# Weight loads one unit later in the order of the DMA queue, and FoX stack pieces at one per step of a product

## What is computed

```python
def first_block(x, ...):
    h = rmsnorm(x, ln1)
    u_pool, gq, gk, gv, gg, ga, fq, fk, fv, ff = split(h @ w_in)
    y_pool = pool_mixer(u_pool, w_pool, pool_scale)            # trailing means
    y_gla = gla_mixer(gq, gk, gv, gg, ga, w_a_up, b_a, gla_gn) # chunked gated linear attention
    y_fox = fox_mixer(fq, fk, fv, ff, b_f)                     # softmax(qk + F_t - F_s), causal, 8 heads of 64
    x = x + concat(y_pool, y_gla, y_fox) @ w_o
    gate, up = split(rmsnorm(x, ln2) @ w_gu)                   # 2 x 2816
    x = x + (silu(gate) * up) @ w_down
    return rmsnorm(x, ln_f)

def second_block(x, ...):
    (q_lat, c_kv, k_rope, z_a, q_b, k_b, v_b, z_b,
     q_idx, k_idx, w_idx, gate_a, gate_b) = split(rmsnorm_2(x, norm_g) @ w_in_2)
    y_a = mla_attention(...) * silu(z_a)   # from the normed latents q_lat and c_kv
    score = sum over heads of w_idx * relu(q_idx . k_idx)   # top 128 keys of each query
    y_b = dsa_attention(...) * silu(z_b)   # attention over those keys, with a T5 bias
    merged = sigmoid(gate_a) * (y_a @ w_o_a) + sigmoid(gate_b) * (y_b @ w_o_b)
    return rmsnorm_2(x + merged @ w_out, final_g)
```

## Time and profile before

| | |
|---|---|
| runs | 1107.45, 1107.36, 1106.17 us; median 1107.36 |
| the profiled execution | 1106.37 us, of which the span of the trace is 1104.6 |
| granted TensorE clock over the span | 0.988 of full speed |
| PE busy | 1050.1 us (95% of the span), 5160 matmuls |
| DVE, ACT, POOL busy | 623.3, 469.3, 256.6 us |
| chain of work that ended last | PE 73%, DVE 14%, ACT 6%, issue 4% |
| loads of weights | 162 of 512 KB, 3.4 us median from issue to landing |

### The profile page before, as it was taken

How to read it: one execution, slowest core, us unless ns; L and a number is a source line. 1 busy time by engine, 2 the same in 40 slices (tenths; PEclk the granted TensorE clock), 3 DMA queues, 4 the chain that set the end, 5 groups by cost and what they waited for, 6 DMA issues and landing times.

```text
span 1104.6 us, 13494 instructions
## 1 busy us (share of the span) xinstructions
PE 1050.1 (95%) x5160; PEld 843.1 (76%) x5160; DVE 623.3 (56%) x1048; ACT 469.3 (42%) x815; POOL 256.6 (23%) x155
## 2 busy tenths in 40 slices
PE   7799889899999999999999998799999999999996
PEld 5597677667888888888888776577787766788885
DVE  6755577747454433344444556898756665425544
ACT  6634346546322222132334465545764554423322
POOL 0581332222101000011113323422323223321100
PEclk9999899999999999999999999999999999999998
DMA  8031132212223232223233326212222423122222
GB/s 293 4 122 50 39 117 78 78 58 77 96 96 96 98 131 77 94 83 109 93 100 94 110 70 209 85 39 74 60 88 78 118 91 104 59 96 96 99 73 77
DMA packets 34655, 102.32 MB, mean 93 GB/s; under 512 B 4544, under 2 KB 8016, under 8 KB 34592
## 3 DMA queue, kind: packets, MB, share of 16 engines
q1 hardware_dynamic: 34592, 101.47, 28.3%
HBM read 93.35 MB, written 4.74 MB: 89 GB/s over the span
## 4 chain that ended last, share of the span: by engine, by line
PE 73%; DVE 14%; ACT 6%; issue 4%; SPq 2%; DMA 1%; DVEq 0%; POOL 0%; ACTq 0%; POOLq 0%
PE bank L1352 20%; PE bank L1354 20%; PE bank L1353 20%; PE bank L1484 2%; PE bank L1475 2%; PE bank L1364 1%; DVE m L2038 1%; DVE score L2029 1%; PE bank L1366 1%; PE bank L1365 1%; DVE score L2040 1%; ACT WH L1537 1%; DVE f_s L1828 1%; DVE small L1922 1%; PE bank L1456 1%
## 5 line engine op out<-in xcount | busy, mean ns | idle before, releaser
L1352 PE MATMUL bank<-HH,WH 128*128 128x512 f32 x808 | 330.1, 409 | 16.9 <-DVE WL L1784 8.3
L1354 PE MATMUL bank<-HH,WL 128*128 128x512 f32 x808 | 317.8, 393 | 0.0
L1353 PE MATMUL bank<-HL,WH 128*128 128x512 f32 x808 | 317.4, 393 | 0.0
L2115 POOL TENSOR_TENSOR WL<-WS,WH 128x1024 fp32r<-128x1024 f32 x64 | 154.8, 2419 | 358.1 <-ACT WH L1537 357.7
L1352 PEld LDWEIGHTS bank<-HH,WH 128*128 128x128 f32 x808 | 154.2, 191 | 54.4 <-DVE WL L1784 8.3
L1537 ACT ACTIVATE WH<-WS 128x1024 fp32r<-128x1024 f32 x162 | 168.6, 1047 | 56.5 <-PE bank L1354 41.5
L1354 PEld LDWEIGHTS bank<-HH,WL 128*128 128x128 f32 x808 | 153.1, 189 | 33.4
L1353 PEld LDWEIGHTS bank<-HL,WH 128*128 128x128 f32 x808 | 153.8, 190 | 29.5 <-issue 1.0
L1784 DVE TENSOR_TENSOR WL<-WS,WH 128x1024 fp32r<-128x1024 f32 x98 | 130.3, 1335 | 25.9 <-ACT WH L1537 25.9
L2168 POOL TENSOR_TENSOR fa<-fa,fg 128x512 f32<-128x512 f32 x22 | 28.3, 1285 | 273.4 <-DVE fa L1975 273.4
L1352 PE MATMUL bank<-GH,WH 128*128 128x512 f32 x176 | 68.5, 389 | 0.0
(11 more groups left out here) (339 smaller groups left out, 1749.7 us busy)
## 6 DMA issues: line engine op xcount, KB each, us to landing
WS<-wall SPq DMA_DIRECT2D x162, 512.0 KB, 3.4
scratch<-rows SPq DMA_DIRECT2D x8, 320.0 KB, 5.6
X<-xT SPq DMA_DIRECT2D x8, 256.0 KB, 6.2
b_t<-scratch SPq DMA_DIRECT2D x8, 256.0 KB, 3.8
outT<-X SPq DMA_DIRECT2D x8, 256.0 KB, 2.1
b_m<-b_m SPq DMA_DIRECT2D x11, 128.0 KB, 4.1
f_s<-f_s SPq DMA_DIRECT2D x8, 128.0 KB
f_m<-f_m SPq DMA_DIRECT2D x8, 128.0 KB
```

The lines of the kernel that those rows point to most:

```text
L1352: e.matmul(b[:, :], wh, xh[:, at_k, :], start=k == 0, stop=False)
L1353: e.matmul(b[:, :], wh, xl[:, at_k, :], start=False, stop=False)
L1354: m = e.matmul(b[:, :], wl, xh[:, at_k, :], start=False, stop=k == n - 1)
L2115: e.tensor_tensor(WL[:, u % NW, :], WS[:, u % NST, :], f32(WH[:, u % NW, :]), ALU.subtract).then_inc(*tick(w_low_g, u))
```

## The change

Two edits. The load of unit u+3 no longer stands at step "split u" in SP's order, but at step "split u+1". Its own wait, for `split_low(u)`, and its buffer stay as they are. And `now["per"]` is not raised to 2.0 behind the gate products: it stays at 1.0 until it is set to 0.0 at the end of FoX.

```diff
@@ build, FoX @@
         run(gate_products())
-        now["per"] = 2.0
         behind.append(fox_stack(1))
         behind.append(gla_out())
@@ sync_program @@
                 elif kind == "split":
-                    load(s["u"] + NST)
+                    if s["u"]:
+                        load(s["u"] - 1 + NST)
                 elif kind == "forget":
```

## The result

The changed kernel takes 1113.91 us (median of 6 runs, 1112.80 to 1116.18); the kernel before, run beside it, 1107.49 us (6 runs, 1106.17 to 1110.57). The ratio is 1.0057, 95% interval 1.0041 to 1.0072: 6.3 us slower, between 4.5 and 8.0. The forecast was 1114.2 us, 1108 to 1120, and slower with 0.79.

A forecast was written before the change was run, and what follows sets the result against it. TensorE, busy 1050.1 of 1104.6 us, was taken as the bound, so only its waits count. 1106.4 + 12.5 (load 104) - 3.4 (DSA copies) - 0.3 (FoX wait) - 1.0 (pieces) = 1114.2 us, range 1108 to 1120.

The forecast's parts named there:

- The block of 31 issues: Between splits 101 and 102 on SP: load 104 goes out behind 24 index and 7 key copies, everything behind 12.5 us later.
- The direct stall of PE: PE waits before the token sums for the copy of the index weights queued behind split 104 on ACT: 7.4 us.
- the bounds: For load 104's delay: 7.4 us if only the direct stall counts, 13.7 if ACT makes nothing good.
- The small copies of DSA: PE's waits at 891.39 and 924.44 go, as copies no longer queue behind loads: 3.4 us gained (0 to 3.95).
- FoX's wait of 0.28 us: PE's wait at 145.05 goes: 0.3 us gained.
- The pieces: FoX, stack pieces at 1.0: 4.0 us gained at f_v, Pb and PT, 3.0 lost; together -1.0 us.
- the new waits: PE waits for stacks 2 and 3 at logits (4,0) and (6,0) in FoX: 1.5 us each, 3.0 in sum.
- The range of -6.5 to +4: Range in us given for the pieces' -1.0, from a gain of 0 to 6.5 and a loss of 0 to 7.
- Load 8: Waits for three copies of the forget rows, lands near 51: costs nothing, or some 4 us without cover.
- the cover: ACT's next split waits 7.83 us for load 9, until 57.31, anyway, which hides the later load 8.
- the hidden load: Rival: load 104, issued by 657.7, reaches ACT in time, and the kernel is faster: 1101.7 us, chance 0.07.
- The partial absorption: Rival: of load 104's delay only the direct 7.4 us stay: 1109.1 us, chance 0.15.

The follow-up runs named there:

- load 104 alone: The kernel before with only the load of unit 104 put behind the 31 issues: 1.0118 of the kernel before, 13.1 us slower.
- the version with load 104 ahead of the block: Both edits, but the load of unit 104 put back ahead of the 31 issues: 0.9942 of the kernel before, 6.4 us faster.
- the run with an 8.1 us delay: Both edits, with the load of unit 104 behind the 24 index copies and ahead of the 7 of the keys: 1.0017 of the kernel before.
- the five profiles: Profiled executions of five with DSA's loads in their old place, two of them the kernel before: 49.71 to 53.37 us from ACT's split 130 to 136.
- two pairs of kernels: Pieces at 1.0 against 2.0, all other loads late: 1.0057 against 1.0062 with load 104 late too, 0.9942 against 0.9960 with it ahead of the block.
- part 2 alone: The kernel before with only the pieces at 1.0 a step, loads as before: 1.0089 of the kernel before, 9.9 us slower.

## Why the prediction was right, step by step

The time was forecast at 7.8 us over the profiled execution of before, and the medians differ by 6.4. That the forecast 1114.2 lies only 0.3 us from the measured 1113.91 is in part luck: the base of 1106.4 was 1.1 us under the median of the kernel before, and the difference was 1.4 too large. The steps, each with what it measured:

- **The block of 31 issues**: forecast +12.5, measured +13.2 in the profile and 13.1 with load 104 alone. The landing took 672.34 - 668.46 = 3.88 us, forecast 3.9. The split came at 672.34 instead of 674.2, since all that precedes it was 0.95 earlier and the seven keys took 4.39 us instead of 5.34. The direct stall of PE was 6.25 us for a forecast 7.4, by the same shift. Split 105 came at 684.36 and was forecast at 686.8: 11.1 us of delay against split 102. The 2 us that then come on top, up to unit 112, the forecast did not have: 1.5 us of them show in the version with load 104 ahead of the block as well (+1.5 between units 108 and 112), and so they do in the second profile of the kernel before, where nothing was changed. In both the granted clock over 711 to 731 was 0.91, and 0.85 in the changed kernel, against 1.00 in the first profile of before. So what load 104 itself costs in the profile is nearer to 11.6 than to 13.2, while the medians say 13.1 and 12.7, each with some 2 to 2.5 us of uncertainty; the bounds were 7.4 and 13.7. (The upper bound counts the 1.0 us of the split itself once too often: from start to start the whole delay is 674.25 - 661.55 = 12.7. And four of the eight ReLUs stand ahead of split 105, not all eight; the chain that was added up has it right.) The choice between them was the step on which the number hung. It was made by following the chain until the delay stopped shrinking, and the run with an 8.1 us delay showed that it was right.
- **The small copies of DSA**: forecast -3.4, measured -2.4 in the profile and -4.6 in the median. The mechanism was right: both copies come in time, the first because it goes out earlier, the second because it takes at most 2.68 us (forecast 2.5). 1.4 of 3.95 us came back at the turning of Pc and at PT, of which I had taken off only 0.5. The clock behind the waits, which by the five profiles makes up the difference between 2.4 and 4.6, was not thought of.
- **FoX's wait of 0.28 us** at 145.05 is gone, as forecast.
- **The pieces**: forecast -1.0, measured -0.5 and -2.0 in two pairs of kernels (each with some 2.5 us of uncertainty), so its sign is not shown. Named waits: those for f_v fell by 2.8 (forecast 1.8), for Pb by 0.5 (1.2), for PT by 0.7 (1.0); the new waits were 1.64 us at logits (4,0) and 2.29 at (6,0), 3.9 for a forecast 3.0. The working had the copy of the k half come last; at (4,0) it was the low half on DVE, which the working left out. In sum FoX's waits (without the one for acc) fell by 1.2 us, and yet the stretch is even: over 205 to 220, where the 2.29 us wait lies, the granted clock was 0.89, and 1.00 before. What that costs no run separates. What was not seen is that this term holds only beside part 1. The price of 1.5 us for a stack that is written just in time took SP to be free for its copies; without the late loads it is 5.5 and 4.4. The range of -6.5 to +4 was narrower than its own terms (a loss of 7 without a gain is +7), and part 2 alone, at +9.9, lies outside both. The forecast is right for the change as a whole, and its working would have given a wrong answer for part 2 alone.
- **Load 8**: forecast nothing, with up to 4 us if the cover fails. Split 8 came 3.0 us later and split 9 no later than the splits ahead of it (ACT waited 2.87 and 4.85 us for the two loads, in place of 7.83 for the second). PE met one wait of 0.76 us at 64.56 that the kernel before did not have, but between units 5 and 16 the kernel loses only 0.03 us (+0.61 and +0.64 against before). So it costs nothing that the profile shows. In all ACT now waits eight times for loads, 26.8 us, in place of the earlier trace rows; 11.64 of them are load 104.
- **The rivals**: the hidden load was excluded by 20 us of issues, as forecast; with the load 12 issues into the block that rival's point (issued by 657.7) is met, and its time comes: 0.9949 of 1107.49 is 1101.8, for a forecast 1101.7. The partial absorption (1109.1) is out by the runs with load 104.

The Trainium skill (DMA: Bandwidth & Descriptors, Rules for kernel authors) says to issue a DMA early. These runs bear it out for load 104, and limit it: on one queue in order, a load that must still wait for its buffer holds up every copy behind it, and DSA was 4.6 us faster with its loads later. Early enough was what counted: 12 issues later cost nothing here.

## What to carry to other kernels

Where one queue issues everything in order, place each transfer by two questions: when its consumer needs it, and what its own wait holds up behind it; a load goes ahead of a long block of issues and behind the small copies that are ready first. The price of a late transfer is the delay of the engine that consumes it, followed until the delay stops shrinking, and not the first stall of the busiest engine. Price parts of a change in the company that they will have: here one part cost 0.9% alone and nothing beside the other.

## What was not expected of the hardware

Two executions of one kernel, with the same order and, in DSA, waits alike to half a us, differ by 4.3 us in their span, and 3.7 of that lie where the granted clock fell to its lower level (1.2 GHz) behind two waits of about 2 us (0.57 and 0.58 over 4 us, in which PE started 16 and 14 matmuls instead of 24 and 19). Here such a wait of PE cost its own length, and in three of five profiled executions some 1.7 to 1.9 us more for each fall behind it. The Trainium skill (TensorE: Matmul & The Clock Gate, section HAM oscillation — how this bites in real kernels) tells of a kernel whose waits for DMA, of some 3 to 5 us, leave the next products on the slow clock; here waits of 1.9 and 2.7 us did so in one execution of the kernel before, and waits of 1.74 and 2.21 us did not in the other.
